# Six norm scales of a decoder layer: sums as columns of token tiles, reciprocals on 3 or 6 columns, spread back by identity products

## The reference, cut to what matters

```python
def _rms(x):
    return x * lax.rsqrt(jnp.mean(x * x, axis=-1, keepdims=True) + EPS)

def block(x, ...):                       # one layer, DEPTH = 1
    x = x + 0.5 * rmsnorm(swiglu(rmsnorm(x, g0), w1, w3, w2), g1)      # FFN 1
    mo = mixer(rmsnorm(x, g2), ...)      # W_in -> mLSTM heads | S5 | short conv -> W_out
    x = x + rmsnorm(mo, g3)
    x = x + 0.5 * rmsnorm(swiglu(rmsnorm(x, g4), w1', w3', w2'), g5)   # FFN 2
```

## Time and profile before

| | us |
|---|---|
| median of 3 runs | 1144.94 (1142.96 to 1145.26) |
| the profiled execution | 1144.65 |
| its span in the trace | 1142.6 |
| PE busy | 1079.3 (94%), 8815 matmuls |
| DVE busy | 564.1 (49%) |
| ACT busy | 341.7 (30%) |
| POOL busy | 98.9 (9%) |

### The profile page before, as it was taken

The page is one execution under the profiler, slowest core; times in us unless marked ns, Lnnn a source line. Parts: engine busy times, 40 slices in busy tenths (PEclk is TensorE's granted clock), DMA queues, the critical chain, the costliest instruction groups (busy, mean ns, idle before and its releaser), DMA issues.

```text
span 1142.6 us, 21300 instructions
## 1 busy us (share of the span) xinstructions
PE 1079.3 (94%) x8815; PEld 1064.3 (93%) x8815; DVE 564.1 (49%) x939; ACT 341.7 (30%) x474; POOL 98.9 (9%) x175
## 2 busy tenths in 40 slices
PE   6999999999999988799999789989999999999994
PEld 6899999999999977799999779989999999999994
DVE  6534433433233479665446957953323333333348
ACT  6222123222222334311432323532221222122231
POOL 0000716900000000310002100000000000000000
PEclk9999999999999999899999989999999999999998
DMA  6222322222222331123312146022233223322232
GB/s 227 78 89 92 92 77 89 92 92 79 88 78 83 97 94 37 38 75 90 116 59 75 4 66 214 24 74 77 89 92 92 77 89 92 92 78 89 83 84 79
DMA packets 31920, 97.95 MB, mean 86 GB/s; under 512 B 5880, under 2 KB 8184, under 8 KB 31864
## 3 DMA queue, kind: packets, MB, share of 16 engines
q1 hardware_dynamic: 31864, 97.17, 28.2%
HBM read 92.46 MB, written 4.70 MB: 85 GB/s over the span
## 4 chain that ended last, share of the span: by engine, by line
PE 82%; DVE 12%; ACT 2%; issue 2%; DMA 1%; DVEq 0%; SPq 0%; ACTq 0%
PE ps L1834 71%; PE ps L1857 2%; PE ps L2224 2%; PE ps L1887 2%; DVE x L1064 1%; DVE y L1060 1%; DVE xl L1069 1%; DVE bcs L1052 1%; DMA raw<-w 1%; DVE bcs L1000 1%; PE ps L2025 1%; DVE wl L876 1%; ACT wh L477 0%; DVE acc L1040 0%; PE ps L2075 0%
## 5 line engine op out<-in xcount | busy, mean ns | idle before, releaser
L876 DVE TENSOR_TENSOR wl<-raw,wh 128x1024 fp32r<-128x1024 f32 (+1 forms) x149 | 183.1, 1229 | 470.7 <-ACT wh L477 470.2
L1834 PE MATMUL ps<-xh,wh 128*128 128x272 f32 x1680 | 352.6, 291 | 20.3 <-DVE xl L985 10.6
L1834 PE MATMUL ps<-xl,wh 128*128 128x272 f32 x1680 | 349.5, 290 | 0.0
L1834 PE MATMUL ps<-xh,wl 128*128 128x272 f32 x1680 | 348.3, 289 | 0.0
L477 ACT CAST wh<-raw 128x1024 fp32r<-128x1024 f32 (+1 forms) x149 | 154.7, 1038 | 455.1 <-PE ps L1834 449.0
L1834 PEld LDWEIGHTS ps<-xh,wh 128*128 128x128 f32 x1680 | 265.7, 190 | 22.2 <-issue 18.6
L1834 PEld LDWEIGHTS ps<-xl,wh 128*128 128x128 f32 x1680 | 266.9, 190 | 0.0
L1834 PEld LDWEIGHTS ps<-xh,wl 128*128 128x128 f32 x1680 | 265.2, 190 | 0.0
L1834 PE MATMUL ps<-hh,wh 128*128 128x272 f32 x608 | 126.4, 289 | 0.5 <-DVE hl L897 0.5
L1834 PE MATMUL ps<-hl,wh 128*128 128x272 f32 x608 | 125.4, 287 | 0.0
L1834 PE MATMUL ps<-hh,wl 128*128 128x272 f32 x608 | 125.3, 287 | 0.0
(11 more groups left out here) (442 smaller groups left out, 1102.9 us busy)
## 6 DMA issues: line engine op xcount, KB each, us to landing
raw<-w SPq DMA_DIRECT2D x120, 512.0 KB, 3.5
raw<-win SPq DMA_DIRECT2D x25, 512.0 KB, 3.5
raw<-w SPq DMA_DIRECT2D x16, 384.0 KB, 3.1
raw<-wout SPq DMA_DIRECT2D x8, 512.0 KB, 4.0
x<-xT SPq DMA_DIRECT2D x4, 544.0 KB, 6.0
o_yT<-x SPq DMA_DIRECT2D x16, 136.0 KB, 1.7
cs<-cT SPq DMA_DIRECT2D x4, 516.0 KB, 4.4
o_sC<-cs SPq DMA_DIRECT2D x4, 516.0 KB, 5.8
```

The source lines that it names most:

```text
L876: V.tensor_tensor(wl[par][:, 0:cols], raw[par][:, 0:cols], wh[par][:, 0:cols].bitcast(F32), ALU.subtract).then_inc(split_done, 1)
L1834: last = mm(ps[:, bank + s, 0:HALF], w[:, kk * P:(kk + 1) * P], a[:, kk, s * HALF:(s + 1) * HALF], start=(kk == 0 and i == 0), stop=(kk == ...
```

## The change

Sums, roots and reciprocals of all nine places (three norms in, three norms out in two halves) move from "all tokens on columns, the same on each partition" to "tokens on partitions". PE multiplies each piece of 128 columns of `acc`, as the stationary operand, with a column of ones: 3 pieces for a half, the last overlapping (`COL_AT`), give 128x3 in PSUM, 6 for all tokens. DVE makes the variance (128x3 or 128x6), ACT the root, DVE the reciprocal. Then PE spreads it back: the column of `stat`, repeated over 128 columns as the stationary operand, times the identity, gives every partition the scales of 128 tokens (`spread_of`). `post_step` reads the scale of y directly from PSUM; on the way in ACT copies it from four banks to `bcs` or `msc` (`input_copy`). `ones2`, `ev` and `input_var` go; `input_scale` makes the epsilon term on 128x6. At b = 1 the variance is now a step of DVE.

Two orders change with it. In `boundary`, each half leaves PSUM ahead of the next low part, the third low part is made behind the last `sq_add`, and on ACT `half_sq(2)` goes ahead of the third split. In the mixer, `gates(s)` goes behind the copies of `bus`.

```diff
@@ ACT
-            def input_root(stage, dst):
-                act.wait_ge(sum_done, 3 * stage + 1)
-                for to, src in upper(dst):
-                    ins = nc.scalar.activation(to, src, ACT.Sqrt, scale=1.0 / D_MODEL, bias=stat[:, 50:51])
-                ins.then_inc(sd_ready, 1)
+            def input_root(stage):
+                act.wait_ge(var_post, 3 * stage + 1)
+                nc.scalar.activation(six(S_R), six(S_VAR), ACT.Sqrt).then_inc(sd_ready, 1)
+            def input_copy(stage, dst):
+                act.wait_ge(r_spread, 3 * stage + 1)
+                to = halves(dst)
+                nc.scalar.copy(to[:, :, 0:P], ps[:, 0:4:2, HALF:HALF + P])
+                nc.scalar.copy(to[:, :, P:HALF], ps[:, 1:4:2, HALF:2 * HALF - P]).then_inc(r_copied, 1)
...
                 half_sq(b, 1)
+                half_sq(b, 2)
                 if b < 2:
...
                     split_to(u2 + 2, third_w[b][0], u1 + 2)
-                half_sq(b, 2)
                 half_sq(b, 3)
...
                 if s == 4:
-                    input_root(1, msc)
-                gates(s)
+                    input_root(1)
+                    input_copy(1, msc)
                 if s == 6:
                     act.wait_ge(bu_s, 1)
...
+                gates(s)
@@ DVE
-            def input_scale(stage, dst, sd):
-                dve.wait_ge(sd_ready, 3 * stage + 1)
-                link(V.reciprocal(dst, sd))
-            def input_var():
-                note(V.scalar_tensor_tensor(ev[:], ev[:], EPS, ev[:], ALU.mult, ALU.mult))
+            def input_scale(stage):
+                dve.wait_ge(sum_done, 3 * stage + 1)
+                V.tensor_scalar(six(S_VAR), ps[:, 0, HALF + P:HALF + P + 6], 1.0 / D_MODEL, EPS, ALU.mult, ALU.add)\
+                    .then_inc(var_post, 1)
+                dve.wait_ge(sd_ready, 3 * stage + 1)
+                V.reciprocal(six(S_R), six(S_R)).then_inc(r_ready, 1)
...
-                link(V.reciprocal(bcs[:, part(s)], bcs[:, part(s)]))
+                V.reciprocal(three(S_R, s), three(S_R, s)).then_inc(r_ready, 1)
...
+                if k == 0:
+                    dve.wait_ge(r_spread, 3 * b + 2 + s)
                 if k < KD:
-                    note(V.tensor_tensor(y[:, k, c], y[:, k, c], bcs[:, c], ALU.mult))
+                    note(V.tensor_tensor(y[:, k, c], y[:, k, c], ps[:, TAIL_BANKS[b][6 * s + 1], 0:HALF], ALU.mult))
@@ PE
+                        if i == 5 and kk == 2:
+                            post_spread(b, 0)
...
+            def sums_of(s, bank, at):
+                for n, lo in enumerate(COL_AT):
+                    ins = mm(ps[:, bank, at + n:at + n + 1], acc[:, s * HALF + lo:s * HALF + lo + P], ones, start=True, stop=True)
+                return ins
+            def spread_of(n, bank, at, w):
+                return mm(ps[:, bank, at:at + w], stat[:, S_R + n:S_R + n + 1].to_broadcast([P, P]), ident[:, P - w:P], start=True,
+                          stop=True)
...
+                        if s == 0 and kk == 3:
+                            post_spread(b, 1)
...
-                unit(fourth_w, 6, KD, xh, xl, lambda kk: input_sums(sums) if kk == 5 else None)
+                unit(fourth_w, 6, KD, xh, xl, lambda kk: sums_inside(kk, sums, b + 1))
...
                         input_sums(KD)
-                        up(u0, hb, 2)
+                        up(u0, hb, 2, lambda kk: input_spread(0) if kk == 3 else None)
```

More of the change, by code:

```diff
@@ L61 @@
 EVENTS = WHOLE + 2 * (KD - WHOLE)
-UPPER = ((0, 240), (240, 480), (480, T))
+COL_AT = (0, P, HALF - P)
+S_VAR, S_R, S_EV = 0, 16, 24
 PRM = {}
@@ L272, in part, with three, six @@
             return slice(s * HALF, (s + 1) * HALF)
-        def upper(dst):
-            return ((dst[:, 0:480].rearrange("p (a c) -> p a c", a=2), ps[:, 0:2, HALF:512]), (dst[:, 480:T], ps[:, 2, HALF:HALF + 64]))
+        def three(at, s):
+            return stat[:, at + 3 * s:at + 3 * s + 3]
+        def six(at):
+            return stat[:, at:at + 6]
         def row(r, a=0, b=T):
@@ L307, in build @@
         sd_ready = sem("sd_ready")
+        r_ready = sem("r_ready")
+        r_spread = sem("r_spread")
+        r_copied = sem("r_copied")
         stat_done = sem("stat_done")
@@ L528, in ffn @@
                         split(u0 + 2, u0 % 2, half(2))
-                        input_root(0, ev)
+                        input_root(0)
                         split(u0 + 3, (u0 + 1) % 2, half(3))
+                        input_copy(0, bcs[:])
                         silu(hb, 0)
@@ L533, in ffn @@
                     else:
-                        input_root(2, ev)
+                        input_root(2)
+                        input_copy(2, bcs[:])
                         nc.scalar.activation(stat[0:1, 62:63], stat[0:1, 62:63], ACT.Silu)
@@ L595, in inputs @@
                     square(x[:, kk], lambda: None)
-            def input_root(stage, dst):
-                act.wait_ge(sum_done, 3 * stage + 1)
-                for to, src in upper(dst):
-                    ins = nc.scalar.activation(to, src, ACT.Sqrt, scale=1.0 / D_MODEL, bias=stat[:, 50:51])
-                ins.then_inc(sd_ready, 1)
-            def post_root(b, s):
-                if b == 1:
-                    act.wait_ge(sum_done, 3 * b + 2 + s)
-                    src = ps[:, TAIL_BANKS[b][6 * s], 0:HALF]
-                    nc.scalar.activation(bcs[:, part(s)], src, ACT.Sqrt, scale=1.0 / D_MODEL, bias=stat[:, 50:51]).then_inc(sd_ready, 1)
-                else:
-                    act.wait_ge(var_post, b + s + 1)
-                    nc.scalar.activation(bcs[:, part(s)], bcs[:, part(s)], ACT.Sqrt).then_inc(sd_ready, 1)
+            def input_root(stage):
[6 more added lines that the diff above has]
+                nc.scalar.copy(to[:, :, P:HALF], ps[:, 1:4:2, HALF:2 * HALF - P]).then_inc(r_copied, 1)
+            def post_root(b, s):
+                act.wait_ge(var_post, 3 * b + 2 + s)
+                nc.scalar.activation(three(S_R, s), three(S_VAR, s), ACT.Sqrt).then_inc(sd_ready, 1)
             def whole_sq(b, m):
@@ L925, in ffn @@
                         lo_part(u0 + 2, u0 % 2)
-                        input_scale(0, bcs[:], ev[:])
+                        input_scale(0)
                         lo_part(u0 + 3, (u0 + 1) % 2)
+                        dve.wait_ge(r_copied, 1)
                         up_first(hb, 0, u0)
                         up_second(hb, 0, u0 + 1, 0)
-                        input_var()
                     else:
-                        input_scale(2, bcs[:], ev[:])
+                        input_scale(2)
+                        dve.wait_ge(r_copied, 3)
                         up_first(hb, 0, u0)
@@ L1859, in half_units, with post_spread, input_spread, sums_inside @@
                     ins.then_inc(z_done if i < 4 else unit_used, 1)
+            def sums_of(s, bank, at):
[5 more added lines that the diff above has]
+                          stop=True)
             def post_sums(b, s):
                 pe.wait_ge(ysq_used, EVENTS * b + WHOLE + 4 * s + 6)
-                mm(ps[:, TAIL_BANKS[b][6 * s], 0:HALF], ones2[:], acc[:, part(s)], start=True, stop=True).then_inc(sum_done, 1)
+                sums_of(s, TAIL_BANKS[b][6 * s], 0).then_inc(sum_done, 1)
+            def post_spread(b, s):
+                pe.wait_ge(r_ready, 3 * b + 2 + s)
+                bank = TAIL_BANKS[b][6 * s + 1]
+                spread_of(3 * s, bank, 0, P)
+                spread_of(3 * s + 1, bank, P, P)
+                spread_of(3 * s + 2, bank, 2 * P, HALF - 2 * P).then_inc(r_spread, 1)
             def input_sums(n):
                 pe.wait_ge(xsq_used, n)
-                for i, (a, z) in enumerate(UPPER):
-                    ins = mm(ps[:, i, HALF:HALF + z - a], ones2[:], acc[:, a:z], start=True, stop=True)
-                ins.then_inc(sum_done, 1)
+                sums_of(0, 0, HALF + P)
+                sums_of(1, 0, HALF + P + 3).then_inc(sum_done, 1)
+            def input_spread(stage):
+                pe.wait_ge(r_ready, 3 * stage + 1)
+                for s in range(2):
+                    spread_of(3 * s, 2 * s, HALF, P)
+                    spread_of(3 * s + 1, 2 * s + 1, HALF, P)
+                    ins = spread_of(3 * s + 2, 2 * s + 1, HALF + P, HALF - 2 * P)
+                ins.then_inc(r_spread, 1)
+            def sums_inside(kk, n, stage):
+                if kk == 4:
+                    input_sums(n)
+                if kk == 6:
+                    input_spread(stage)
             def enter(b, sums):
```

32 lines of the change are left out of this document (17 added, 15 removed).

## The result

| | before | changed |
|---|---|---|
| median, us | 1144.18 (4 runs) | 1129.66 (4 runs, 1128.59 to 1130.52) |
| ratio, 95% interval | | 0.9873 (0.9856 to 0.989) |
| profiled execution, us | 1144.65 | 1128.59 |
| its span | 1142.6 | 1126.6 |
| PE busy | 1079.3 (94%) | 1084.7 (96%) |

The change makes the kernel 14.5 us (1.3%) faster by the medians and 16.06 us by the two profiled executions. The forecast was 1125.6 with a range of 1121.5 to 1133.5: the range holds the time, and the gain was put a third too high.

A forecast was written before the change was run, and what follows sets the result against it. PE was taken as the bound (busy 94% of 1142.6 us), plus its gaps and the slow clock behind them. Gains 1.1 + 5.35 + 7.6 + 4.2 + 1.1 = 19.35 us gave 1125.3, forecast 1125.6 us, range 1121.5 to 1133.5.

The forecast's parts named there:

- A: Start of FFN 1: the 2.74 us gap closes while PE arrives 1.6 later; gain 1.1 us (0.6 to 1.7).
- D: Boundary 2: the wide reciprocal shrinks, so the second half's scaling starts earlier; gain 1.1 us (0.5 to 1.6).
- the prices: PE's new pieces at each norm: three sums 0.67 us, six 1.33; three spreads 0.62, six 1.25.
- the PSUM operand: `post_step` multiplies y by a scale in PSUM, 48 times; nothing booked, though the skill's rule gives some 3 us.
- Rivals 3 and 5: 3: PSUM operand costs what the errata says, 1128.3, chance 0.04. 5: new sums and spreads cost more, slower, chance 0.03.
- B1: Boundary 0 to the mixer's first evacuation: earlier sums and no wide reciprocals; gain 5.35 us (4.3 to 6).
- Rival 6: DVE and ACT wait for spreads as long as for reciprocals; only `bus` gains: about 1142 to 1144, chance 0.03.
- rival 4: Better: the 2.4 us gap at boundary 0 stays warm (1.7 us), or spreads are cheaper: 1122 to 1124, chance 0.08.
- B2: Mixer's first units: the 4.16 us `bus` wait and slow clock go; gain 7.6 us (3.5 to 8.5).
- C: Boundary 1 to FFN 2's fifth unit: shorter gaps, no slow clock behind them; gain 4.2 us (0.8 to 4.6).
- The clock terms: Slow clock lost behind four gaps, booked as regained when gaps shrink to 1.65 us or less: 7.7 us in all.
- rival 1: The clock stays low although gaps shrink: all four terms fail, 1133.3; two fail, 1129; chance 0.20.

The follow-up runs named there:

- (b) alone: The kernel before with only the new order of `boundary` on DVE and ACT (evacuations ahead of low parts, third low part behind the last addition): 1141.5 us.
- (c) alone: The kernel before with one edit: in the mixer ACT makes the copies of `bus` ahead of `gates(s)`; 1138.25 us, ratio 0.9938.
- (a) alone: The changed kernel with both orders put back, leaving only the norms with tokens on partitions and the spreads: 1140.27 us, ratio 0.9962.
- the first fills: The changed kernel with zero products in two gaps, 9 before boundary 0's first sums and 6 before boundary 1's second sums: 1129.95 us, ratio 0.9868.

## Why the prediction was right in its direction and too high in its size

- **A, D, the prices, the PSUM operand.** As forecast (1.3 for 1.1, 1.1 for 1.1). Rivals 3 and 5 are out: 427 ns for the PSUM operand, 0.21 to 0.23 us for a product. The Trainium skill (VectorE: DVE Perf Modes, "The TRN2 errata") gives an operation 62 cycles more with a PSUM source than with SBUF sources; no row here shows them.
- **B1.** The first sums came 2.7 us earlier (2.5 forecast), and the first evacuation 5.1 (5.35). PE's new wait in `enter` was 0.43 for 0.55. Rival 6 is out, and rival 4 with it: the clock fell behind the gap at boundary 0 in every profile that has it open.
- **B2.** 7.9 for 7.6. The clock came back in the first unit and in the chunks, and M6's low part had just enough slack. The Trainium skill (SBUF — State Buffer, "Who interferes with whom") says that a VectorE instruction with two SBUF inputs contends with a GpSimd one that reads SBUF. The rows agree in kind: 0.3 to 0.4 us for an operation, 2.0 us for the chain.
- **C, the step that failed.** Of the 4.2 us, 1.0 was for the fourth unit's earlier start, 1.5 for the way from there to the fifth unit and 1.7 for the clock behind it. The second came (1.35), the first turned into -0.8 and the third into 0.6. The first rested on "short, so clock loss goes". The gap did shrink to 1.31 us, as forecast at 1.2, but the clock behind it fell all the same, here and in every other profile with this gap open: from 711.4 us on PE ran at the low level, the spread took 1.13 us instead of the 0.62 booked, and DVE waited 1.84 us for it. With the gap filled the fourth unit came 0.8 us earlier instead of 0.8 later. The third part did come at first (1.53) and then lost 0.93 us in front of a low part, 0.67 of it as idle time, because silu's table now stood behind ACT's copies. I had named just that in A and not carried it over to C. Also, that the loss behind the fifth unit was there to be won is chance: (b) alone and (c) alone have the same gap of 3.00 us and no loss behind it.
- **The mixer's end.** Forecast to move as a whole, it gave back 0.5 us: the clock was low for longer at 640 (3.06 for 1.71), with nothing changed in its instructions.
- **The clock terms.** I booked four of them, 7.7 us. Three of the four places did lose their loss (6.0 us), one did not, and the total fell by 4.3 us in one execution and by 2.3 in the other. This is rival 1 in part: one term failed, not the two for which it gave 1129, and that the time came out at 1129.66 is partly luck, since the rest of the miss is C's wait, the mixer's end and the pattern of the execution. The row that I took for a threshold, 1.65 us with full clock behind it, is no rule for another place: it was free there in each profile of the old norms, while 1.31 us in front of the new sums cost 1.71 each time, and 2.32 us at boundary 1 was free twice and cost 1.7 once.

## What to carry to other kernels

A term for the clock is not a price that the length of a gap sets: one place lost the same in eight profiles of eight, others in one of three. Look at the same place in more than one profile before you book it, add the losses up over the execution, since one that leaves one gap may come back behind the next, and count what lies beside a wait as nothing. When an edit shortens one step of a chain over three engines, look at what another of them did for nothing beside the old long step (here a table load under a reciprocal). And a gain upstream ends at the next wait that another engine releases, as (a) alone lost 1.2 us at `bus` until (c) moved that release.

## What I had not expected of the hardware

- The granted clock was 0.5 in busy stretches with no gap ahead of them (533.9 and, with the gaps filled, 492.9), each behind 2.7 us or more of products on 4 of the 128 partitions, and two executions of one program differed by 2.0 us in what the low level cost (12.3 and 14.3), with three of the places different.
- Behind gaps filled with products that add zero the granted clock was 1.00 each time: at boundary 0 (one profile), at boundary 1 and at the mixer's end (two each, the middle gap there still 1.74 us long). Whether the loss goes for good or turns up elsewhere differed by place: with the first fills it came back at 445 and 492.9, and with those at the mixer's end it did not.
- POOL beside DVE costs both: 0.71 to 1.09 us for DVE's operation of 544 columns on 4 partitions, 0.62 to 1.10 for POOL's of 256 columns on 128.
